# Decoder step with a mixture of experts: the order of a gather and an addition on GpSimd in the periods of the second to fourth expert

## The chip, the cores and the metric

The kernel runs on one core of one Trainium2 chip. The metric is the device time of one execution in microseconds, here the median of several runs of the same kernel. All times come from the profiled execution of the kernel or from those runs. Lines (L749, or line 749) are lines of the kernel file.

## What is computed

The reference is one layer of a hybrid decoder, for a prompt group (512 rows) and a sample group (8 x 4 rows) that share the weights: attention with a window, a short gated convolution and attention over a memory, their normalised concatenation times W_out, and then a mixture of 32 experts of which each row picks four. All of it is float32. What matters here is the last part:

```
h  = x + mix @ w_out
hn = rmsnorm(h)                                  # 544 rows of 1024
gates, experts = softmax(top4(hn @ w_router + b_router))
for each expert e, on the rows that picked it:
    g = hn @ w_gate_up[e] + b_gate_up[e]         # 1024 x 2048, interleaved gate and up
    a = (clip(up, -7, 7) + 1) * gate' * sigmoid(1.702 * gate'),  gate' = min(gate, 7)
    y[row] += gate_of_row * (a @ w_down[e] + b_down[e])
y = rmsnorm(h + y)
```

## The kernel before

The layer up to the router takes the first 250 us or so. Then come 32 experts in order, each with up to 104 rows (a branch with more blocks stands behind a flag and isn't taken here). The rows hn lie in a DRAM table (hn_tbl), and the result is summed up in another (y_tbl), which begins with h.

**A period.** Each expert n has a period, period(n), written out by hand on each engine. Its weights are 12 MB: four chunks of 2 MB for gate and up and two for down, each used as two halves, so 12 halves a period (HALVES). TensorE counts each used half up in `w_used`. Each half is split in two float32r parts, high (ScalarE, high_part, L1133) and low (VectorE, low_part, L1754), and TensorE multiplies three of the four combinations (products, L2435 to L2437). SyncE loads a chunk as soon as TensorE has used up what lay in its buffer. The halves of a period are shifted by two: period n begins with half 2 of expert n and takes in halves 0 and 1 of expert n + 1 as its steps i = 8 and 9. Between the halves TensorE transposes the activations (act_rows, L2430) and, at step 5, the gathered rows of the next expert (x_rows, L2419).

**The rows of an expert.** For the first ten experts the indices of expert n + 2 come from small matrix products (info) at the end of step 9 of period n, and VectorE writes them to idx_i (slot_info, L1721, at step 10). GpSimd then gathers the rows (gather, L749, an indirect DMA of 104 rows of 4 KB). Later experts take the indices from a table. The result of expert n - 1 leaves PSUM on ScalarE at step 0 (y_rows, L1143), and GpSimd adds it to y_tbl by an indirect DMA that adds (scatter, L762). The additions to y_tbl are made one after the other, each behind the landing of the one before, as they may hit the same rows.

**The down offsets.** The offsets b_down are not added expert by expert. For a row tile j of 128 rows (j = 0 to 3; j = 4 has 32) TensorE multiplies the gates of the tile with all experts' down offsets (bias_term, L2482), ScalarE copies the result from PSUM to SBUF (bias_evict, L1270), and GpSimd adds it to y_tbl (add_bias, L814). This happens in the first experts: tiles 0 and 1 before and in period 0, and tile n + 1 in periods n = 1 to 3. Tiles 0, 2, 3 and 4 share one buffer, bias4, so that bias_evict of tile j waits for the addition of the tile before:

```
if j >= 2:
    ac.wait_ge(sem(f"bias_added{0 if j == 2 else j - 1}"), 16)
```

On ScalarE bias_evict(n + 1) stands at step 1 of period n, behind the split of the half of step 4, and ahead of gate_over (L1149) and gate_sigmoid (L1155) of step 2 and of the later splits. On VectorE the product with the sigmoid (swiglu, L1836) waits for gate_sigmoid. TensorE waits for the same bias_evict ahead of step 4 (the term uses a PSUM bank of the transposes). GpSimd's scatter(n) waits for the addition of tile n (n = 1 to 3), and period 4 for that of tile 4.

**GpSimd's own order.** It also spreads the gate and up offsets of the next expert over 128 partitions: bias_rows(n, part), two broadcasts of 512 columns (L682) for each part. They wait for SyncE's load of one row (load_biases, L518), which SyncE issues once ScalarE has written the row before into PSUM (bias_seed, L1171). And in periods 2 to 6 it writes a table of slots with four indirect DMAs a period (table_rows, L733), which the later experts read. slots (L716) copies a column for info.

Of the kernel before, what the change touches and what calls it, by code (L numbers as in the profile page):

```python
# [52 lines left out]
UB = 4  # L53
# [59 lines left out]
def build(nc, x_prompt, x_sample, mem_prompt, cache_win_k, cache_win_v, win_kT, mem_kT, cache_mem_v,  # L113
# [4 lines left out]
    with ctx:  # L118
# [13 lines left out]
        def sem(name):  # L132
            if name not in sems:
                sems[name] = ctx.enter_context(nc.semaphore(name))
            return sems[name]
# [192 lines left out]
        def bias_row(j):  # L328

            return yrow[:, 1, :] if j == 1 else bias4  # L330
# [14 lines left out]
        def row_tile(r):  # L345
            return (memrow[:, r, :], P) if r < 2 else (xrow[0:ROWS[r - 2], r - 2, :], ROWS[r - 2])
# [293 lines left out]
        def _(pool):  # L640
# [6 lines left out]
            for r in range(7):  # L647
                n = row_tile(r)[1]
# [25 lines left out]
            def bias_rows(n, part):  # L674

                pool.wait_ge(sem(("ld_vec_bias0", "ld_mck_bias1")[part]), n * 16 + 32)
                if not isinstance(n, int):
                    seen = cst[0:1, 0:NVC * (3 + part)].rearrange("p (e c) -> p e c", c=3 + part)
                    nc.gpsimd.tensor_copy(arrived[0:1, part:part + 1], seen[:, bass.ds(n, 1), 0])  # L679
                for half in range(2):  # L680
                    cols = slice(part * D + half * 512, part * D + (half + 1) * 512)
                    nc.gpsimd.partition_broadcast(brow[:, cols], brow[0:1, cols], channels=P).then_inc(sem("bias_cast"), 1)  # L682
# [30 lines left out]
            def slots(n, k):  # L713

                wait(pool, "info_pe", counted(n) - 1)
                nc.gpsimd.tensor_copy(rv[:, k % 2], rv_all[:, bass.ds(n, 1)].rearrange("p o j c -> p (o j) c")).then_inc(sem("rv_ready"), 1)  # L716
                pool.wait_ge(sem("rv_ready"), n)
# [8 lines left out]
            def table_rows(first, last):  # L726

                pool.wait_ge(sem("ld_gffn"), 32)
                pool.wait_ge(sem("slot_rows"), 1)
                pool.reg_add(bound, none, CAP * NE - 1)  # L730
                for i in range(first, last):
                    n = ROWS[i // TOPK]
                    nc.gpsimd.indirect_dma_start(  # L733
                        slot_tbl[:, :], bass.IndirectOffsetOnAxis(ap=slot_i[0:n, i:i + 1].bitcast(U32), axis=0),
                        slot_row[0:n, i, :], None, bounds_check=bound, oob_is_err=False).then_inc(sem("table"), 16)

            def table_slots(n, k):

                pool.wait_ge(sem("ld_cst"), 32)
                nc.gpsimd.tensor_copy(idx_i[0:CAP, k % UB:k % UB + 1], slot_sb[0:CAP, bass.ds(n, 1), 0])  # L740
                nc.gpsimd.tensor_copy(gcol[0:CAP, k % UB:k % UB + 1], slot_sb[0:CAP, bass.ds(n, 1), 1]).then_inc(sem("rv_ready"), 1)
                pool.wait_ge(sem("rv_ready"), n)

            def gather(n, k, table=False):

                if not table:
                    pool.wait_ge(sem("idx_ready"), counted(n) + 1)
                pool.reg_add(bound, none, NT - 1)
                nc.gpsimd.indirect_dma_start(  # L749
                    xg[0:CAP, k % 2, :], None, hn_tbl[:, :],  # L750
                    bass.IndirectOffsetOnAxis(ap=idx_i[0:CAP, k % UB:k % UB + 1].bitcast(U32), axis=0),
                    bounds_check=bound, oob_is_err=False).then_inc(sem("gathered"), 16)

            def scatter(n, k):

                pool.wait_ge(sem("yrow_ready"), n * 2)
                if isinstance(n, int) and 0 < n <= 3:
                    for j in ((0, 1) if n == 1 else (n,)):
                        pool.wait_ge(sem(f"bias_added{j}"), 16)
                wait(pool, "scattered", n * 16 - 16)  # L760
                pool.reg_add(bound, none, NT - 1)
                nc.gpsimd.indirect_dma_start(  # L762
                    y_tbl[:, :], bass.IndirectOffsetOnAxis(ap=idx_i[0:CAP, (k - 1) % UB:(k - 1) % UB + 1].bitcast(U32), axis=0),
                    yrow[0:CAP, (k - 1) % 2, :], None,
                    bounds_check=bound, oob_is_err=False, compute_op=ALU.add).then_inc(sem("scattered"), 16)
# [13 lines left out]
            def period(n, k, last=False, table=False, bare=False, overflow=False):  # L779
                old = not (last or table or bare)  # L780
                if old:
                    slots(n + 2, k)
                if not isinstance(n, int) or n > 0:
                    scatter(n, k)
                if not last:
                    if overflow:
                        bias_rows(n + 1, 0)
                    bias_rows(n + 1, 1)
                    pool.wait_ge(sem("w_used"), n * HALVES + 9)
                if isinstance(n, int) and 0 < n < UB:  # L790
                    pool.wait_ge(sem("scattered"), n * 16)
                    add_bias(n + 1)
                if table:
                    table_slots(n + 2, k + 2)
                if old or table:
                    gather(n + 2, k + 2, table)
                if old and not overflow or table:
                    bias_rows(n + 2, 0)
                if old and isinstance(n, int) and 2 <= n < 7:
                    table_rows(4 * (n - 2), 4 * (n - 1))  # L800

# [8 lines left out]
            def add_bias(j):  # L810

                pool.wait_ge(sem("bias_row"), 2 * j + 2)
                pool.reg_add(bound, none, NT - 1)
                nc.gpsimd.indirect_dma_start(  # L814
                    y_tbl[:, :], bass.IndirectOffsetOnAxis(ap=row_i[0:ROWS[j], j:j + 1].bitcast(U32), axis=0),
                    bias_row(j)[0:ROWS[j], :], None,
                    bounds_check=bound, oob_is_err=False, compute_op=ALU.add).then_inc(sem(f"bias_added{j}"), 16)
# [4 lines left out]
            for u in range(2 * UB):  # L822
                if u == UB:
                    pool.wait_ge(sem("bias_added4"), 16)
                period(u, u)
            with pool.Fori(2, NE // UB - 1) as it:
                for u in range(UB):
                    period(it * UB + u, u, table=True)
# [24 lines left out]
            for u in range(UB):  # L853
                period(NE - UB + u, u, u == UB - 1, u < 2, u == 2)
# [1759 lines left out]
```

## Time and profile before

| what | us |
|---|---|
| median of 3 runs (1393.88 to 1400.48) | 1394.35 |
| the profiled execution | 1399.39 |
| its span | 1397.5 |
| TensorE busy in the span | 1359.8 |
| VectorE busy | 1206.0 |
| ScalarE busy | 1070.6 |
| GpSimd busy | 759.1 |

The profile is of one execution. In it period 2 runs from about 331.2 to 366.9 us by TensorE's first and last product, period 4 from 402.6 to 449.1, period 5 to 484.0. In its rows PE is TensorE, PEld its weight loads, DVE VectorE, ACT ScalarE, POOL GpSimd and SP SyncE. A row of a timeline gives the start in us from the span's start, the duration in us, engine, line, operation, output and input tile, the count, and in brackets the idle time before it with what ended that. The landing of a DMA is counted from the start of its issue. Several buffers are parts of one tile named area, so area<-hn_tbl,idx_i is the gather, y_tbl<-area,idx_i the scatter of an expert's result and y_tbl<-area,row_i the addition of a row tile.

### The profile page before, as it was taken

What the parts mean: (1) busy time and instruction counts of PE and PEld (TensorE: products, weight loads), DVE (VectorE), ACT (ScalarE), POOL (GpSimd) and SP (SyncE); (2) the same over time, 40 slices, a digit from 0 to 9 for tenths busy, and PEclk for the clock granted to TensorE, in tenths of its full rate; (3) what the DMA queues carried; (4) which work ended last, traced back from release to release, by engine and by line L of the source; (5) the groups of instructions that cost most, each with busy time, mean ns of one, the idle gap of its engine ahead of it and who ended that gap; (6) DMA issues with size and microseconds to landing.
All of it is one profiled execution on the core that took longest, in us unless ns stands there. A gap on an engine that the chain in (4) does not pass through costs nothing.

```text
span 1397.5 us, 19410 instructions
## 1 busy us (share of the span) xinstructions
PE 1359.8 (97%) x6775; PEld 1000.4 (72%) x6775; DVE 1206.0 (86%) x1098; ACT 1070.6 (77%) x1102; POOL 759.1 (54%) x363
## 2 busy tenths in 40 slices
PE   9999998999997999999999999999999999999995
PEld 6988655667775777777777777777777777777773
DVE  5466555899996999999999999999999999999996
ACT  5354413878885888888888888888888888888884
POOL 2022112386775979656666666566665666665403
PEclk9999999999998999999999999999999999999998
DMA  9522171999997999999999999999999999999984
GB/s 353 196 66 83 75 286 61 367 378 372 388 391 269 363 386 364 366 387 382 381 390 388 369 385 369 382 384 376 383 381 370 383 376 378 391 376 377 383 304 149
DMA packets 52506, 461.48 MB, mean 330 GB/s; under 512 B 11545, under 2 KB 15611, under 8 KB 26825
## 3 DMA queue, kind: packets, MB, share of 16 engines
q1 hardware_dynamic: 40169, 438.59, 80.2%
q0 software_dynamic: 10624, 20.42, 6.5%
q10 hardware_dynamic: 1648, 1.65, 0.4%
q8 instruction: 36, 0.59, 0.2%
q14 instruction: 29, 0.24, 0.0%
HBM read 446.88 MB, written 24.31 MB: 337 GB/s over the span
## 4 chain that ended last, share of the span: by engine, by line
PE 67%; DMA 2%; issue 1%; POOL 1%; DVE 0%; ACT 0%; POOLq 0%; ACTq 0%; DVEq 0%
PE psum L2437 21%; PE psum L2436 21%; PE psum L2435 21%; PE psum L2419 1%; PE psum L2430 1%; DMA area<-hn_tbl,idx_i 1%; POOL small L840 0%; DMA y_tbl<-area,idx_i 0%; POOL brow L682 0%; DVE low L1754 0%; PE psum L2406 0%; DVE ring L1900 0%; POOL out L850 0%; ACT area L1202 0%; ACT ring L1210 0%
## 5 line engine op out<-in xcount | busy, mean ns | idle before, releaser
L1754 DVE TENSOR_TENSOR low<-raw,high 128x2048 fp32r<-128x2048 f32 x384 | 868.2, 2292 | 36.8 <-ACT high L1133 36.7
L1133 ACT CAST high<-raw 128x2048 fp32r<-128x2048 f32 x384 | 727.8, 1912 | 39.0 <-PE psum L2437 35.0
L2435 PE MATMUL psum<-high,area_r 128*104 128x512 f32 x1536 | 610.8, 398 | 3.8 <-DVE area_r L1823 1.5
L2437 PE MATMUL psum<-low,area_r 128*104 128x512 f32 x1536 | 604.7, 394 | 0.0
L2436 PE MATMUL psum<-high,area_r 128*104 128x512 f32 x1536 | 604.3, 393 | 0.0
L2437 PEld LDWEIGHTS psum<-low,area_r 128*104 128x104 f32 x1536 | 258.2, 168 | 96.7
L2435 PEld LDWEIGHTS psum<-high,area_r 128*104 128x104 f32 x1536 | 258.4, 168 | 95.9 <-DVE area_r L1818 2.1
L2436 PEld LDWEIGHTS psum<-high,area_r 128*104 128x104 f32 x1536 | 258.6, 168 | 91.0
L682 POOL PARTITION_BROADCAST brow<-brow x128 | 253.1, 2047 | 27.8 <-issue 15.0
L749 POOL DMA_INDIRECT area<-hn_tbl,idx_i x32 | 173.5, 5423 | 71.7 <-DVE idx_i L1721 42.6
L679 POOL COPY arrived<-cst 1x1 f32 x40 | 84.8, 2121 | 123.0 <-DMA brow<-in_biases 123.0
L762 POOL DMA_INDIRECT y_tbl<-area,idx_i x31 | 110.7, 3571 | 39.1 <-ACT area L1143 27.1
L740 POOL CAST idx_i<-us 104x1 int32 (+1 forms) x22 | 17.8, 807 | 135.9 <-PE psum L2437 135.9
L1159 ACT CAST area_r<-psum 128x416 fp32r<-128x416 f32 x64 | 32.4, 506 | 73.3 <-PE psum L2430 73.3
L659 POOL TENSOR_TENSOR ring<-ring,small 128x512 f32<-128x512 f32 (+2 forms) x18 | 24.2, 1358 | 111.5 <-DVE small L1425 111.5
L1171 ACT COPY psum<-brow 104x512 f32<-104x512 f32 x128 | 75.5, 591 | 0.0
L1149 ACT ACTIVATE area<-psum,cst 104x512 f32<-104x512 f32 x64 | 44.1, 689 | 29.7 <-PE psum L2437 29.7
L733 POOL DMA_INDIRECT slot_tbl<-wr,us x20 | 50.8, 2538 | 5.4 <-issue 5.4
L2196 PE MATMUL psum<-ring,area 128*128 128x512 f32 x112 | 52.4, 601 | 0.0
L1823 DVE TENSOR_TENSOR area_r<-psum,area_r 128x416 fp32r<-128x416 f32 x64 | 37.5, 587 | 15.5 <-ACT area_r L1159 15.4
L1155 ACT ACTIVATE area<-area,cst 104x512 f32<-104x512 f32 x64 | 47.0, 735 | 2.8
L1143 ACT ACTIVATE area<-psum,area 104x512 f32<-104x512 f32 x62 | 39.3, 686 | 12.8 <-PE psum L2437 12.8
(287 smaller groups left out, 1229.5 us busy)
## 6 DMA issues: line engine op xcount, KB each, us to landing
raw<-in_w_gate_up SPq DMA_DIRECT2D x128, 2048.0 KB, 12.2
raw<-in_w_down SPq DMA_DIRECT2D x64, 2048.0 KB, 11.7
ring<-in_w_in SPq DMA_DIRECT2D x7, 1024.0 KB, 16.2
ring<-in_x_prompt SPq DMA_DIRECT2D x8, 512.0 KB, 9.6
ring<-in_w_out SPq DMA_DIRECT2D x7, 512.0 KB, 4.4
ring<-in_w_mem_kv SPq DMA_DIRECT2D x2, 1024.0 KB, 9.4
ring<-in_mem_kT SPq DMA_DIRECT2D x1, 2048.0 KB
ring<-in_cache_mem_v SPq DMA_DIRECT2D x1, 2048.0 KB, 8.4
```

What stands on the lines that cost most here:

```text
L679: nc.gpsimd.tensor_copy(arrived[0:1, part:part + 1], seen[:, bass.ds(n, 1), 0])
L682: nc.gpsimd.partition_broadcast(brow[:, cols], brow[0:1, cols], channels=P).then_inc(sem("bias_cast"), 1)
L733: nc.gpsimd.indirect_dma_start(slot_tbl[:, :], bass.IndirectOffsetOnAxis(ap=slot_i[0:n, i:i + 1].bitcast(U32), axis=0), slot_row[0:n, i, : ...
L749: nc.gpsimd.indirect_dma_start(xg[0:CAP, k % 2, :], None, hn_tbl[:, :], bass.IndirectOffsetOnAxis(ap=idx_i[0:CAP, k % UB:k % UB + 1].bitca ...
L762: nc.gpsimd.indirect_dma_start(y_tbl[:, :], bass.IndirectOffsetOnAxis(ap=idx_i[0:CAP, (k - 1) % UB:(k - 1) % UB + 1].bitcast(U32), axis=0) ...
L1133: nc.scalar.copy(high_w(i), raw_w(t)).then_inc(sem("w_high"), 1)
L1171: nc.scalar.copy(banks[q][0:CAP, :], brow[0:CAP, q * 512:(q + 1) * 512]).then_inc(sem("spare_bias_in"), 1)
L1754: v.tensor_tensor(low_w(t), raw_w(t), high_w(i), ALU.subtract).then_inc(sem("w_low"), 1)
L2196: last = mm(bank[0:n, :], zT[:, t, j * P:j * P + n], wo[t][:, half * 512:(half + 1) * 512], start=(t == tiles[0]), stop=(t == tiles[-1]))
L2435: mm(bank, high, wh, start=start, stop=False, skip_group_check=True)
L2436: mm(bank, low, wh, start=False, stop=False, skip_group_check=True)
L2437: return mm(bank, high, wl, start=False, stop=stop, skip_group_check=True)
```

## The change

In the periods of experts 1, 2 and 3 (0 < n < UB, UB = 4), GpSimd's wait for the landing of scatter(n) and add_bias(n + 1) move from ahead of gather(n + 2) and bias_rows(n + 2, 0) to behind them. They stay ahead of table_rows. The operations, their data and all other engines' programs are the same.

```diff
@@ -787,15 +787,15 @@
                         bias_rows(n + 1, 0)
                     bias_rows(n + 1, 1)
                     pool.wait_ge(sem("w_used"), n * HALVES + 9)
-                if isinstance(n, int) and 0 < n < UB:
-                    pool.wait_ge(sem("scattered"), n * 16)
-                    add_bias(n + 1)
                 if table:
                     table_slots(n + 2, k + 2)
                 if old or table:
                     gather(n + 2, k + 2, table)
                 if old and not overflow or table:
                     bias_rows(n + 2, 0)
+                if isinstance(n, int) and 0 < n < UB:
+                    pool.wait_ge(sem("scattered"), n * 16)
+                    add_bias(n + 1)
                 if old and isinstance(n, int) and 2 <= n < 7:
                     table_rows(4 * (n - 2), 4 * (n - 1))
```

## Rows read from the trace of the kernel before

**Rows 1.** The page, busy us of each engine, share of the span, instructions
```profile
PE 1359.8 (97%) x6775; PEld 1000.4 (72%) x6775; DVE 1206.0 (86%) x1098; ACT 1070.6 (77%) x1102; POOL 759.1 (54%) x363
```
**Rows 2.** Waits of PE, 260 to 560 us: total, times, longest
```profile
PE psum L2419 <- DMA area<-hn_tbl,idx_i: 9.6, 1, 9.6
```
**Rows 3.** Busy us of PE, PEld, DVE, ACT, POOL by stretch; clock, DMA share, GB/s
```profile
331.20:366.90 35.70, 35.70 (x169) 26.22 (x168) 35.63 (x27) 30.82 (x29) 25.41 (x8) 1.00 1.02 373
402.60:449.10 46.50, 36.91 (x165) 27.03 (x164) 34.33 (x26) 29.79 (x27) 24.10 (x13) 0.89 0.85 314
449.10:484.00 34.90, 34.90 (x165) 25.80 (x164) 33.58 (x26) 29.85 (x26) 32.53 (x13) 1.00 0.97 360
```
**Rows 4.** Timeline of PE, 418 to 431 us
```profile
428.77 1.65 PE L2419 MATMUL psum<-cst,area 104*128 104x104 f32 x8 [9.60 <-DMA area<-hn_tbl,idx_i]
```
**Rows 5.** Timeline of POOL, 270 to 470 us
```profile
324.28 1.58 POOL L814 DMA_INDIRECT y_tbl<-area,row_i  x1 [7.26 <-issue]
328.03 2.60 POOL L749 DMA_INDIRECT area<-hn_tbl,idx_i  x1 [2.16 <-DVE idx_i L1721]
332.37 3.73 POOL L682 PARTITION_BROADCAST brow<-brow  x2 [1.74 <-DMA brow<-in_biases]
...
355.06 5.85 POOL L814 DMA_INDIRECT y_tbl<-area,row_i  x1 [4.46 <-PE psum L2437]
363.12 7.38 POOL L749 DMA_INDIRECT area<-hn_tbl,idx_i  x1 [2.20 <-DVE idx_i L1721]
370.54 2.76 POOL L682 PARTITION_BROADCAST brow<-brow  x2
...
386.71 1.78 POOL L716 CAST area_r<-area_r 128x20 fp32r<-128x20 f32 x1
389.35 6.33 POOL L762 DMA_INDIRECT y_tbl<-area,idx_i  x1 [0.86 <-POOL area_r L716]
395.13 5.06 POOL L682 PARTITION_BROADCAST brow<-brow  x2
407.96 3.94 POOL L814 DMA_INDIRECT y_tbl<-area,row_i  x1 [7.76 <-PE psum L2437]
412.20 5.17 POOL L749 DMA_INDIRECT area<-hn_tbl,idx_i  x1 [0.30 <-issue]
```
**Rows 6.** Landings of L814 (x5), L762 (x8), L749 (x8), 265 to 560 us
```profile
DMA to landing us min/median/max: 10.0/13.8/18.3
DMA to landing us min/median/max: 8.7/13.2/17.7
DMA to landing us min/median/max: 13.4/16.0/21.6
```
**Rows 7.** Timeline of DVE, 265 to 460 us
```profile
341.43 0.68 DVE L1836 SCALAR_TENSOR_TENSOR area<-psum,area 104x512 f32<-104x512 f32 x1
...
362.08 0.15 DVE L1721 TENSOR_SCALAR idx_i<-psum 104x1 int32<-104x1 f32 x1
...
375.40 0.68 DVE L1836 SCALAR_TENSOR_TENSOR area<-psum,area 104x512 f32<-104x512 f32 x1
...
396.79 0.15 DVE L1721 TENSOR_SCALAR idx_i<-psum 104x1 int32<-104x1 f32 x1
```
**Rows 8.** Timeline of ACT, 270 to 450 us
```profile
338.07 1.08 ACT L1270 COPY area<-psum 128x512 f32<-128x512 f32 x2 [1.90 <-DMA y_tbl<-area,row_i]
...
339.83 0.73 ACT L1155 ACTIVATE area<-area,cst 104x512 f32<-104x512 f32 x1
...
371.90 1.05 ACT L1270 COPY area<-psum 32x512 f32<-32x512 f32 x2
...
373.63 0.73 ACT L1155 ACTIVATE area<-area,cst 104x512 f32<-104x512 f32 x1
```
**Rows 9.** Timeline of SP, 300 to 380 us
```profile
325.01 0.24 SPq L518 DMA_DIRECT2D brow<-in_biases  x1
...
360.62 0.24 SPq L518 DMA_DIRECT2D brow<-in_biases  x1
```

## The prediction

> **What bounds the kernel now.** I read the shares first. TensorE is busy for 97% of the span [rows 1], so this time is set by TensorE, and only what makes it wait, or what removes a wait, can count. Then I asked for TensorE's waits over the first eight experts: there is one long one, 9.6 us, in which the transposes of gathered rows (line 2419) wait for the gather [rows 2]. Then the table by expert [rows 3]: expert 4 (fifth in order) takes 46.5 us of TensorE's time line, expert 5 takes 34.9. The difference, **11.6 us**, is all that the stretch can give back. It is a little more than the wait, because the granted clock of that stretch is 0.89 of full speed on average: the first transposes after the wait take 1.65 us for eight [rows 4].
>
> Why is this gather late? In period 3 GpSimd reaches the scatter of expert 3 at 389.35, ends the spreading of offsets at 395.13 + 5.06 = 400.19, and then nothing runs until 407.96 [rows 5]. The releaser named there is TensorE, but by the code three waits stand in a row, the last for the scatter's landing: 389.35 + 17.7, the longest landing of line 762 in the experts asked for [rows 6], is 407.05. Only then come the row tile's addition at 407.96 and the gather at 412.20. Its indices had been ready since 396.79 + 0.15 [rows 7]. So 15 us pass between the indices and the gather, and 12.0 of them (400.19 to 412.20) are the wait and the addition that the change moves behind it.
>
> **What the change moves.** No instruction is added or removed. In periods 1, 2 and 3 the wait for the scatter and the addition (its wait, its descriptors, its transfer) go behind the gather and behind two broadcasts, which have waits of their own: the gather waits for the indices that VectorE writes late in the period, the broadcasts for a row of offsets that SyncE loads.
>
> **Period 3, the gain.** GpSimd would be free at 400.2 in the old frame, after the indices. The gather goes out about 11.8 us earlier, lands after the 16.5 us that it took (rows wanted at 428.77 - 9.60 = 419.2; 400.4 + 16.5 = 416.9), 2.3 us ahead of the need [rows 4, 5]. I take the whole 11.6 us as gained; at the longest landing of a gather in the stretch, 21.6 us [rows 6], 2.8 us of wait would stay.
>
> **Periods 1 and 2, the price.** The addition has a customer that the gather doesn't: one buffer (bias4) holds row tile 2, then 3, then 4. ScalarE may write tile 3 (bias_evict, line 1270, at the second step of period 2) only when the addition of tile 2 has landed. This wait shows already, 1.90 us, until 338.07 [rows 8]; the addition went out at 324.28 and took 13.8. In period 3 the same write starts at 371.90 with no idle time shown. Both stand at their edge, so each microsecond by which the addition is later falls on ScalarE nearly whole. Behind the write on ScalarE stand the clip and sigmoid of SwiGLU and all following splits.
>
> *Period 1.* The gather stays where it is, at 328.03, as it was bound by its indices and not by the addition. The broadcasts stay at 332.37, since they wait for the row of offsets (issued by SyncE at 325.01, 7.36 us before [rows 9]), and end at 336.1. The addition goes out at 336.3, 12.0 us later than before. For its landing I take 13.8 us, which is both its own and the median of the five additions [rows 6]: 350.1. The write moves from 338.07 to 350.1. What does that do to the end? VectorE is the one to follow, not TensorE: it is busy 35.63 of 35.70 us in this period [rows 3], so lost time on it isn't made up. Its SwiGLU product starts at 341.43 and needs ScalarE's sigmoid, which ended at 339.83 + 0.73 = 340.56, so 0.87 us is spare [rows 7, 8]. Shift: 350.1 - 338.07 - 0.87 = **11.2 us**. TensorE stops ahead of the fifth of the period's twelve half-chunks (it waits there for the same write, since that shares a PSUM bank), due near 331.2 + 35.7 x 4/12 = 343.1, and again for a split half that ScalarE and VectorE have not made yet.
>
> *Period 2*, all of it 11.2 later. Indices at 362.08 + 11.2 = 373.3, gather at 374.3 (363.12 before), its descriptors 7.38 us, until 381.7; the offsets' row would be there at 360.62 + 11.2 + 7.36 = 379.2, so the gather decides; the broadcasts add 2.76, and the addition goes out at 384.7 [rows 5, 7, 9]. Landing: 13.8 again, 398.5. The write of tile 4 was at 371.90, with 375.40 - 374.36 = 1.04 us spare ahead of VectorE's product [rows 7, 8]. Whole shift by then: 398.5 - 371.90 - 1.04 = **25.6 us**.
>
> *Period 3* pays no third time: no tile comes after 4. Here GpSimd must still be in time: after 384.7 up to 5.9 us of descriptors, the four table scatters (370.54 + 2.76 to 386.71, so 13.4), the slots 1.8, the scatter 6.3 and the broadcasts 5.1, which ends near 418. The indices come at 396.8 + 25.6 = 422.4 [rows 5, 7]: the gather isn't late. Behind it, in period 4, GpSimd first waits for the addition of tile 4; the broadcasts for the next expert then come near to their need, which may cost 0 to 5 us. I take nothing and leave the 5 to the range.
>
> **Sum.** +25.6 - 11.6 = +14.0 us. Against the profiled execution's own time, 1399.39 (span 1397.5 and 1.9 around it), that is 1413.4. The median of the runs is 1394.35, 5.0 less; I carry the difference over: **1408**. The unprofiled runs might hold less of the old wait for the gather than this one does; then the gain is smaller and the result higher.
>
> **The landing of the moved addition is the unknown cost.** With L for it, the two periods give about 2L - 2.0 (13.8 gives 25.6). The nearest rows are 10.0 and 18.3, the shortest and longest addition [rows 6]. At 10.0, with short descriptors of 2.6 us for the gather (that of 328.03) so that the offsets' row decides, the shift is 15.4 and the sum +3.8, 1398. At 18.3 with the same 7.38 it is 34.6 and the sum +23, 1417. I take 13.8, because TensorE's stop does not stop the weights already asked for: in the stop of the old kernel the gather still took 16.5. Break-even is at L = 6.8 us, and no indirect transfer of these experts landed under 8.7.
>
> The Trainium skill has a rule that speaks for a quick landing: "DMA: Bandwidth & Descriptors", section "Anatomy of one DMA — SWDGE (gpsimd) path", fits a GpSimd transfer as 2.0 us plus its bytes over 436 GB/s. For a tile of 128 rows of 4 KB that would be an estimated 3.2 us, and the sum by it -7, or 1387. The trace does not agree: a transfer of this size took 13.8 [rows 6].
>
> **Rivals.**
> - *The addition lands at once, the write is hardly held, and the kernel gets faster.* Place: the wait on line 1270 in periods 2 and 3; price 2L - 2.0; it decides from 6.8 us down. ScalarE reached the write at 338.07 - 1.90 = 336.2 [rows 8], and the addition would have to be down soon after its issue at 336.3; with no hold at all the time is 1394.35 - 11.6 = 1383. Against it: the five additions took 10.0 to 18.3, and the wait is there already. Chance 0.05. The fit of the Trainium skill named above would bring this case about.
> - *The holds come, small.* A TensorE that stops asks for no new weights, so transfers drain and land sooner, as the scatter behind the old stop did in 8.7. 8.7 in both periods: 2 x 8.7 - 2.0 = 15.4, or 12.8 with the quick descriptors, less 11.6, so +1 to +4, and 1397 in the middle. Chance 0.15.
> - *The holds come and the gather stays late*, because the scatter, the table's scatters and the gather share GpSimd's queue. No gain then: +25.6, 1420. For it: gathers up to 21.6 us. Against it: 419.2 - 396.9 = 22 us lie between indices and need. Chance 0.10.
> - My forecast, both holds and the gain: 0.70.
>
> **How the numbers follow.** A difference under 0.5% (7 us) is about what a measurement of this kernel can tell from no change. Faster by more: 0.05. Within: the small holds, most of 0.15, and the lower end of the forecast (L under 11.5): 0.17 together. Slower: 0.78. The range goes from the small holds, 1397, to 1419, nearly the case without a gain and L = 18.3.
>
> **What the profile would show.** Right: ScalarE's line 1270 waits for the DMA of the row addition about 14 us in period 2 (1.9 before) and about 15 in period 3 (0 before), TensorE idle some 8 to 10 us in each, mostly ahead of the fifth half-chunk, and again about 2; VectorE idle 11 to 14 us ahead of line 1836; no wait of line 2419 for the gather; periods 2 and 3 near 47 and 50 us, period 4 near 35; from expert 5 on nothing new. Each step has its row: addition 2 issued near 336, addition 3 near 385, gather 5 within 2 us of its indices. Wrong: additions that land in under 7 us; a line 1270 with no wait; a gather of period 3 that TensorE still waits for.

## The result: slower by 1.4%, and the profile after

| | us |
|---|---|
| kernel before, median of 4 runs (1393.88 to 1400.48) | 1396.37 |
| changed kernel, median of 4 runs (1414.22 to 1416.25) | 1414.88 |
| ratio, 95% interval | 1.0138 (1.0111 to 1.0164) |
| profiled execution after, and its span | 1414.22, 1412.4 |

The forecast was 1408 in a range of 1397 to 1419, slower by 14. The loss is 18.5 us by the medians. The spans of the two profiles differ by 14.9 only, because the profile of before was taken of an execution that was slower than most of that kernel's; the section on the spread comes back to it.

The waits of TensorE in the changed kernel, 260 to 620 us (who waited for whom: total, times, longest), are the first thing to read against [rows 2]:

```profile
PE psum L2435 <- ACT area L1270: 17.8, 2, 9.4
PE psum L2435 <- DVE low L1754: 1.5, 4, 0.7
...
PE psum L2419 <- DMA area<-hn_tbl,idx_i: 0.2, 1, 0.2
```

The wait of 9.6 us for the gather is gone. In its place TensorE waits twice, 17.8 us together, for bias_evict. ScalarE and VectorE in the same stretch of the same kernel:

```profile
ACT area L1270 <- DMA y_tbl<-area,row_i: 28.1, 2, 14.6
...
ACT psum L1171 <- POOL brow L682: 10.3, 2, 6.4
```

```profile
DVE area L1836 <- ACT area L1155: 24.1, 2, 13.4
```

So the chain is the forecast one: the addition of a row tile lands late, ScalarE may not write the next tile into bias4, its sigmoid comes late, and VectorE's product and all splits behind it. The second ScalarE line is new: it twice waits for GpSimd's broadcasts. Now the timeline of GpSimd, 270 to 530 us, with the rows that answer to [rows 5]:

```profile
327.12 2.54 POOL L749 DMA_INDIRECT area<-hn_tbl,idx_i  x1 [11.07 <-DVE idx_i L1721]
330.54 4.57 POOL L682 PARTITION_BROADCAST brow<-brow  x2 [0.88 <-DMA brow<-in_biases]
335.29 1.71 POOL L814 DMA_INDIRECT y_tbl<-area,row_i  x1 [0.17 <-issue]
...
373.50 7.33 POOL L749 DMA_INDIRECT area<-hn_tbl,idx_i  x1 [20.92 <-DVE idx_i L1721]
380.87 2.54 POOL L682 PARTITION_BROADCAST brow<-brow  x2
383.58 3.48 POOL L814 DMA_INDIRECT y_tbl<-area,row_i  x1 [0.17 <-issue]
...
433.64 6.17 POOL L814 DMA_INDIRECT y_tbl<-area,row_i  x1 [0.17 <-issue]
...
446.93 5.42 POOL L733 DMA_INDIRECT slot_tbl<-wr,us  x1 [0.30 <-issue]
452.35 1.91 POOL L716 CAST area_r<-area_r 128x20 fp32r<-128x20 f32 x1
455.13 6.01 POOL L762 DMA_INDIRECT y_tbl<-area,idx_i  x1 [0.87 <-POOL area_r L716]
460.58 1.79 POOL L682 PARTITION_BROADCAST brow<-brow  x2
```

The gather of period 1 did not get earlier: before it started at 328.03 [rows 5], and this execution runs 1 us ahead of the other from period 1 on. Only the addition moved. ScalarE, 325 to 540 us, answers to [rows 8]:

```profile
348.76 1.07 ACT L1270 COPY area<-psum 128x512 f32<-128x512 f32 x2 [13.56 <-DMA y_tbl<-area,row_i]
...
396.48 1.05 ACT L1270 COPY area<-psum 32x512 f32<-32x512 f32 x2 [14.56 <-DMA y_tbl<-area,row_i]
...
461.87 0.59 ACT L1171 COPY psum<-brow 104x512 f32<-104x512 f32 x1 [6.36 <-POOL brow L682]
```

And VectorE, 325 to 420 us, to [rows 7]; the products were at 341.43 and 375.40:

```profile
351.27 0.69 DVE L1836 SCALAR_TENSOR_TENSOR area<-psum,area 104x512 f32<-104x512 f32 x1 [10.74 <-ACT area L1155]
...
398.96 0.69 DVE L1836 SCALAR_TENSOR_TENSOR area<-psum,area 104x512 f32<-104x512 f32 x1 [13.36 <-ACT area L1155]
```

They come 9.8 and 23.6 us later, in an execution that is 1 us ahead. For a balance by period I take the starts of y_rows on ScalarE (L1143) one after the other; where the broadcasts hold ScalarE up, only the sum of two periods means something.

| from one y_rows to the next, us | before | after | difference |
|---|---|---|---|
| period 1 | 37.6 | 37.5 | -0.1 |
| period 2 | 35.6 | 46.7 | +11.1 |
| period 3 | 35.6 | 47.7 | +12.0 |
| periods 4 and 5 | 82.0 | 73.8 | -8.2 |
| periods 6 and 7 | 70.5 | 71.5 | +1.0 |
| sum | | | +15.8 |

With the 1 us by which this execution was ahead at its period 1, that is the 14.9 of the spans. From period 8 on both take 34.6 a period.

### The profile page after: what moved, and what is told of

The parts are those of the page before. It is cut to its first block, busy times and chain, and to the rows that moved or that the text cites. A ratio compares the mean times of both kernels' runs of the same rounds, so it can differ in the third digit from the quotient of the medians.

```text
span 1412.4 us, 19413 instructions
## 1 busy us (share of the span) xinstructions
PE 1366.3 (97%) x6775; PEld 1004.4 (71%) x6775; DVE 1204.7 (85%) x1098; ACT 1069.1 (76%) x1102; POOL 743.5 (53%) x363
## 4 chain that ended last, share of the span: by engine, by line
PE 78%; DVE 9%; issue 4%; POOL 3%; DMA 3%; ACT 2%; SPq 0%; POOLq 0%; ACTq 0%; DVEq 0%
PE psum L2435 20%; PE psum L2437 20%; PE psum L2436 20%; DVE low L1754 5%; PE psum L2196 4%; PE psum L2033 2%; PE psum L2035 2%; PE psum L2034 2%; DMA y_tbl<-area,row_i 2%; PE psum L2430 1%; PE psum L2419 1%; POOL brow L682 1%; POOL slot_tbl L733 1%; DMA ring<-in_x_prompt 1%; ACT high L1133 1%
## 5 line engine op out<-in xcount | busy, mean ns | idle before, releaser
L1754 DVE TENSOR_TENSOR low<-raw,high 128x2048 fp32r<-128x2048 f32 x384 | 865.5, 2285 | 42.5 <-ACT high L1133 42.2
L1133 ACT CAST high<-raw 128x2048 fp32r<-128x2048 f32 x384 | 727.1, 1912 | 34.6 <-PE psum L2437 30.5
L2435 PE MATMUL psum<-high,area_r 128*104 128x512 f32 x1536 | 612.8, 399 | 23.3 <-ACT area L1270 17.8
L682 POOL PARTITION_BROADCAST brow<-brow x128 | 236.0, 1915 | 29.5 <-DMA brow<-in_biases 23.3
L749 POOL DMA_INDIRECT area<-hn_tbl,idx_i x32 | 174.5, 5454 | 112.6 <-DVE idx_i L1721 84.0
L762 POOL DMA_INDIRECT y_tbl<-area,idx_i x31 | 105.0, 3388 | 52.7 <-ACT area L1143 27.1
L740 POOL CAST idx_i<-us 104x1 int32 (+1 forms) x22 | 17.8, 808 | 131.9 <-PE psum L2437 131.9
L1836 DVE SCALAR_TENSOR_TENSOR area<-psum,area 104x512 f32<-104x512 f32 x64 | 43.8, 685 | 24.1 <-ACT area L1155 24.1
L1839 DVE SCALAR_TENSOR_TENSOR area<-area 104x512 f32<-104x512 f32 x64 | 47.3, 740 | 2.2
```

What stands on the lines that cost most here:

```text
L749: nc.gpsimd.indirect_dma_start(xg[0:CAP, k % 2, :], None, hn_tbl[:, :], bass.IndirectOffsetOnAxis(ap=idx_i[0:CAP, k % UB:k % UB + 1].bitca ...
L762: nc.gpsimd.indirect_dma_start(y_tbl[:, :], bass.IndirectOffsetOnAxis(ap=idx_i[0:CAP, (k - 1) % UB:(k - 1) % UB + 1].bitcast(U32), axis=0) ...
L1133: nc.scalar.copy(high_w(i), raw_w(t)).then_inc(sem("w_high"), 1)
L1754: v.tensor_tensor(low_w(t), raw_w(t), high_w(i), ALU.subtract).then_inc(sem("w_low"), 1)
L2435: mm(bank, high, wh, start=start, stop=False, skip_group_check=True)
```

## Experiments

Two theories stood against each other. A is the forecast's: the price is the hold on bias4, twice, and the gain is the gather of period 3. B: moving the addition costs by itself, in GpSimd's queue or by late broadcasts, in each of the three periods alike. Each run has its own runs of the kernel before beside it, with medians of 1393.86, 1393.72 or 1393.43 us; against 1393.86 the whole change costs 21.0 us. All edits are to the lines of the change, against the kernel before, unless said otherwise. In kernels with added lines, bias_evict is L1271, L1273 or L1275 and x_rows L2420 to L2424.

### One period at a time

Period 3 alone:

```diff
-                if isinstance(n, int) and 0 < n < UB:
+                if isinstance(n, int) and 0 < n < 3:
                     pool.wait_ge(sem("scattered"), n * 16)
                     add_bias(n + 1)
...
                     bias_rows(n + 2, 0)
+                if isinstance(n, int) and n == 3:
+                    pool.wait_ge(sem("scattered"), n * 16)
+                    add_bias(n + 1)
```

> Only in period 3 do the wait for the scatter and the addition stand behind the gather and the broadcasts; periods 1 and 2 are as before. Theory A (the price is the hold on bias4 in periods 2 and 3, the gain is the gather of period 3 that is no longer late): no tile comes after 4, so there is no price; line 1270 waits 1.9 us as before, no wait of line 2419 for a gather, and the time is 5 to 11 us below the kernel before (ratio 0.992 to 0.996), less than 11.6 because the broadcasts of period 4 come late behind the addition (the changed kernel shows a wait of 6.4 us on them). Rival B (moving the addition costs by itself, through GpSimd's queue or late broadcasts, in every period alike): a third of the loss stays, ratio 1.00 to 1.005.

Measured: 1388.34 us against 1393.86 for before, ratio **0.9961** (0.9946 to 0.9977). This is faster than both kernels. Its waits of TensorE, 260 to 620 us, hold nothing large:

```profile
PE psum L2438 <- DVE area_r L1821: 0.8, 1, 0.8
PE psum L2438 <- issue: 0.6, 1, 0.6
PE psum L2438 <- DVE area_r L1826: 0.2, 1, 0.2
```

and GpSimd, 320 to 530 us, sends the gather as soon as the broadcasts of 394.57 end, 12.4 us earlier than at 412.20 [rows 5], while the addition waits for the scatter as it did before:

```profile
394.57 5.05 POOL L682 PARTITION_BROADCAST brow<-brow  x2
399.81 2.82 POOL L749 DMA_INDIRECT area<-hn_tbl,idx_i  x1 [0.18 <-issue]
403.26 2.31 POOL L682 PARTITION_BROADCAST brow<-brow  x2 [0.63 <-DMA brow<-in_biases]
407.04 1.81 POOL L817 DMA_INDIRECT y_tbl<-area,row_i  x1 [1.47 <-DMA y_tbl<-area,idx_i]
```

The addition goes out at 407.04, where it had been at 407.96. So in period 3 the move is free: the wait for the scatter's landing, not GpSimd's order, sets the addition. B, which wanted a loss here, is out. Periods 4 and 5 take 70.35 us together and periods 4 to 7 take 140.9, and ScalarE waits for no broadcast there, against the expectation.

Period 1 alone (the conditions are 1 < n < UB ahead and n == 1 behind):

> Only in period 1 is the addition behind the gather and the broadcasts. Theory A: one hold, line 1270 waits about 13.5 us in period 2, TensorE loses 11 us there, the gather of period 3 stays late and its wait of some 10 us stays: ratio 1.006 to 1.010. Rival B: a third of the loss, about +5 us, spread and not ahead of the fifth half-chunk, ratio near 1.004.

Measured: 1400.72 against 1393.86, ratio 1.0049 (1.0032 to 1.0067), which is below the 1.006 to 1.010 that A was given and near the number of B. The place decides: ScalarE's timeline, 330 to 420 us, and the waits of TensorE show one hold where A puts it.

```profile
349.63 1.07 ACT L1273 COPY area<-psum 128x512 f32<-128x512 f32 x2 [12.86 <-DMA y_tbl<-area,row_i]
```

```profile
PE psum L2438 <- ACT area L1273: 7.7, 1, 7.7
...
PE psum L2422 <- DMA area<-hn_tbl,idx_i: 0.7, 1, 0.7
```

Period 2 takes 46.1 us, 10.5 more than in the run with period 3 alone. But the wait for the gather in period 4 is down to 0.7, though that gather was not moved here. GpSimd, 325 to 480 us, shows where it went:

```profile
400.43 6.34 POOL L762 DMA_INDIRECT y_tbl<-area,idx_i  x1 [0.86 <-POOL area_r L716]
...
413.91 2.83 POOL L817 DMA_INDIRECT y_tbl<-area,row_i  x1 [2.63 <-PE psum L2440]
417.04 2.63 POOL L749 DMA_INDIRECT area<-hn_tbl,idx_i  x1 [0.30 <-issue]
```

The scatter of expert 3 is issued 11.1 us later than in [rows 5], like all the rest behind the hold, but it lands after 12.6 us in place of 17.7. So the addition goes out only 6.0 and the gather only 4.8 us later than before, and the gather lands after 13.9 in place of 16.5. Why the scatter landed sooner was not tried. In periods 4 to 7 ScalarE waits twice for broadcasts, 3.8 and 3.9 us, and they take 143.8 us, 2.9 more than with period 3 alone. By the periods this run is 10.5 + 2.9 = 13.3 us behind that one, by the medians 12.4. A had left the wait for the gather standing; that it is nearly gone explains the low ratio.

Period 2 alone (n in (1, 3) ahead, n == 2 behind):

> Only in period 2 is the addition behind the gather and the broadcasts. Theory A: one hold, on the write of tile 4 in period 3. The addition goes out some 17 us later than before (355.1 to about 372), so line 1270 waits 13 to 15 us there, and TensorE loses 11 to 13 us in period 3; from this goes what the wait for the gather of period 4 was worth in the runs (about 4 to 5 us by the run with its own buffer and the old order, and by the run with period 3 alone), as the gather is then no longer in time trouble or is: ratio 1.005 to 1.010. Rival B (a third of the loss for each period): 1.0045. Together with the run of period 1 alone and of period 3 alone the three should add up to the whole change within 5 us, or the periods interact.

Measured: 1405.01 against 1393.72, ratio 1.0084 (1.0055 to 1.0112). The addition went out at 374.77, 19.7 later than in [rows 5], ScalarE's write waited 17.2 us, TensorE 12.1, and no wait for the gather is left. The three ratios add up to +0.49 + 0.84 - 0.39 = 0.94%, 13 us, where the whole change costs 1.38%, 19 us. So the periods interact: the wait for the gather, worth 5.5 us by the run with period 3 alone, can be removed only once, but each of the three runs removes it. Against this, the hold of period 3 is longer when it stands alone: the period takes 50.4 us here and 47.7 in the changed kernel.

### A buffer of its own

```diff
-            return yrow[:, 1, :] if j == 1 else bias4
+            return yrow[:, 1, :] if j == 1 else bias_own if j == 3 else bias4
...
-                if j >= 2:
-                    ac.wait_ge(sem(f"bias_added{0 if j == 2 else j - 1}"), 16)
+                if j in (2, 4):
+                    ac.wait_ge(sem(f"bias_added{j - 2}"), 16)
```

To make room, the two buffers of the slot mask (hot) became one, whose write waits for the product before it, and the tile area grew by 136 columns.

> The changed kernel, with a buffer of its own for row tile 3, so that the write of tile 3 waits for no addition and that of tile 4 for the addition of tile 2 only (one of the two buffers of the slot masks is given up for the room). Theory A: both waits on line 1270 go (0 to 2 us left), periods 2 and 3 return to about 35.7 us, and the gain of period 3 stands alone: ratio to the kernel before 0.991 to 0.997. But GpSimd's scatters 2 and 3 still wait for the additions of tiles 2 and 3, and may hold up broadcasts: up to 5 us of ScalarE waiting for line 682 in place of it. Rival B: the loss stays, ratio 1.010 or more.

Measured on the changed kernel's order: 1388.50 against 1393.86, ratio **0.9963** (0.9944 to 0.9981). The whole loss is gone, with GpSimd's order as in the change. ScalarE, 330 to 380 us, writes both tiles with no idle time ahead:

```profile
336.76 1.07 ACT L1271 COPY area<-psum 128x512 f32<-128x512 f32 x2
...
372.71 1.04 ACT L1271 COPY area<-psum 32x512 f32<-32x512 f32 x2
```

In this run ScalarE waits 4.4 us for broadcasts, 3.9 of them at 403.10, within what was allowed for.

The control, with the order of before:

> Control for the one above: the kernel before with the same separate buffer and the single slot mask. Theory A: the 1.9 us wait on line 1270 goes, which VectorE had covered but for 0 to 1 us, and the late gather stays: ratio 0.998 to 1.002. If it is far from 1, the room that was made costs or gives something by itself, and the run above has to be read against this one.

Measured: 1393.62 against 1393.86, ratio 0.9996 (0.9979 to 1.0014). The buffer by itself gives nothing. So the hold on bias4 is the cause of the loss, shown by taking it away: 1.0138 becomes 0.9963. B is out here too: what late broadcasts cost by themselves is a few us at most.

### What sets the landing of the addition

In all three periods, gather, addition, broadcasts:

```diff
                     gather(n + 2, k + 2, table)
+                if isinstance(n, int) and 0 < n < UB:
+                    pool.wait_ge(sem("scattered"), n * 16)
+                    add_bias(n + 1)
                 if old and not overflow or table:
                     bias_rows(n + 2, 0)
```

> In all three periods the order is gather, wait and addition, broadcasts: the addition is behind the gather but ahead of the broadcasts. Theory A with price 2L - 2.0 less what the addition is earlier: it goes out near 330.8 in place of 335.3 in period 1 (4.5 us earlier) and some 2.7 us earlier in period 2, so the waits on line 1270 shrink by that to about 9 and 8 to 12 us, and the time lies 7 to 10 us below the changed kernel: ratio 1.007 to 1.010. If the gather right ahead of it in the same queue lengthens the landing by the same amount, the ratio stays near 1.013 (rival C: the queue's order sets the landing, not the time of issue).

Measured: 1411.64 against 1393.72, ratio 1.0141 (1.0109 to 1.0173). GpSimd and ScalarE in the period of the first hold:

```profile
328.58 2.53 POOL L749 DMA_INDIRECT area<-hn_tbl,idx_i  x1 [11.06 <-DVE idx_i L1721]
331.42 3.28 POOL L814 DMA_INDIRECT y_tbl<-area,row_i  x1 [0.30 <-issue]
...
349.13 1.07 ACT L1270 COPY area<-psum 128x512 f32<-128x512 f32 x2 [12.49 <-DMA y_tbl<-area,row_i]
```

The addition of tile 2 went out at 331.42, 2.8 us behind its gather, but it landed after 17.7 us, at 349.1. In the changed kernel it went out at 335.29 and took 13.5. With the executions' offset of 1.4 us taken out, 5.3 us of earlier issue brought 1.0 us of earlier landing. My price, 2L - 2.0 with a fixed L, was wrong for this run, and rival C came true. By the medians this order is 3.2 us faster than the changed kernel; A had wanted 7 to 10. The gather ahead landed at 328.58 + 13.2 = 341.8, so 7.3 us lie between the two landings; in the changed kernel 7.8 (gather 341.0). This suggested rule D: about 13 us from the issue, or about 7.5 us behind the transfer ahead in this queue, whichever is later. The test takes the gather from ahead of the addition, but leaves the addition as late:

```diff
+                ahead = isinstance(n, int) and 0 < n < 3
+                if ahead:
+                    bias_rows(n + 2, 0)
+                    pool.wait_ge(sem("scattered"), n * 16)
+                    add_bias(n + 1)
                 if old or table:
                     gather(n + 2, k + 2, table)
```

(period 3 as in the change)

> Periods 1 and 2: broadcasts, wait and addition, then the gather; period 3 as in the changed kernel. So the addition is as late as in the changed kernel but has no gather ahead of it in GpSimd's queue. Theory D (a transfer of this queue lands about 13 us after its issue, or about 7.5 us after the one ahead of it, whichever is later; it fits the landings of the changed kernel and of the run with the addition right behind the gather): addition 2 goes out near 335.5 and lands near 348.5, the wait on line 1270 stays at 12 to 14 us in period 2, and about 11 to 13 in period 3, where the gather no longer stands between; ratio 1.010 to 1.014. Rival C (the gather ahead in the queue makes the landing late): addition 2 lands 5 to 7 us sooner, near 342, the waits shrink to 6 to 8 us, ratio 1.002 to 1.006.

Measured: 1405.29 against 1393.43, ratio 1.0091 (1.0060 to 1.0121), between the two. GpSimd, 320 to 450 us, and ScalarE, 330 to 420 us, tell them apart:

```profile
335.30 1.70 POOL L819 DMA_INDIRECT y_tbl<-area,row_i  x1 [0.17 <-issue]
337.30 1.43 POOL L749 DMA_INDIRECT area<-hn_tbl,idx_i  x1 [0.30 <-issue]
...
376.58 3.29 POOL L819 DMA_INDIRECT y_tbl<-area,row_i  x1 [0.18 <-issue]
```

```profile
349.35 1.07 ACT L1275 COPY area<-psum 128x512 f32<-128x512 f32 x2 [14.17 <-DMA y_tbl<-area,row_i]
...
389.61 1.05 ACT L1275 COPY area<-psum 32x512 f32<-32x512 f32 x2 [7.10 <-DMA y_tbl<-area,row_i]
```

In period 1 no other transfer of the queue is under way when the addition goes out, and it still took 14.0 us from 335.30; the hold stays at 14.2. C fails there, and the landing is the one of D. In period 2 the addition went out 7.0 us sooner than in the changed kernel, because it need not wait for the gather's indices and its 7.33 us of descriptors; it took 13.0, and the hold shrank from 14.6 to 7.1. The ratio lies under what was expected of D, since I had overlooked that period 2 gets its addition out earlier; 7 us off the changed kernel's 1.0138 is 1.0088, and 1.0091 was measured.

D is fitted to these rows and is no law of the queue. In the kernel before, the addition of 355.06 took 16.8 us (to 371.88) and the scatter of 389.35 took 17.7, though the landing ahead of theirs in this queue lay over 15 us back; both kept GpSimd busy for about 6 us, which the landing includes, as it is counted from the start of the issue.

### Period 3 alone, with the addition ahead of the broadcasts

> Period 3 alone, with the order gather, addition, broadcasts. Theory A: like the run with period 3 alone and the addition behind the broadcasts, since the scatter's landing near 407 sets the addition in both: ratio 0.995 to 0.998. The broadcasts of period 3 then wait for 407 and end near 414; their customer, the seed of the next expert, comes at about 414 too, so up to 2 us may be lost.

Measured: 1389.99 against 1393.72, ratio 0.9974 (0.9956 to 0.9992): the order within period 3 makes no difference that these intervals can tell. Its profile has a small one: ScalarE waits twice, 3.9 us each, for broadcasts, and periods 4 to 7 take 142.9 us in place of 140.9; the medians differ by 1.7.

### The spread of the kernel before

> The kernel before once more, for a second profile. The runs of before so far spread over 1388 to 1401. Theory: the spread is the length of the wait for the gather in period 4, 9.6 us in the first profile (1399.4) and 3.6 in that of the own buffer with the old order (its span 1393.3). A profile with a time near 1394 should show 3 to 5 us, one near 1399 8 to 10. Rival: the spread is elsewhere (clock, the layer's first part), and the wait is 9 to 10 us whatever the time.

Measured: 1394.36 against 1393.72, ratio 1.0002 (0.9982 to 1.0022). The profiled execution took 1395.40, and TensorE's wait for the gather, 260 to 620 us, is not 9.6 but:

```profile
PE psum L2419 <- DMA area<-hn_tbl,idx_i: 3.8, 1, 3.8
```

Its GpSimd rows, 320 to 450 us, show what differs: the addition and the gather take 1.40 and 2.48 us on GpSimd in place of 3.94 and 5.17 [rows 5], and the gather landed after 13.8 us in place of 16.5.

```profile
408.01 1.40 POOL L814 DMA_INDIRECT y_tbl<-area,row_i  x1 [7.26 <-issue]
409.71 2.48 POOL L749 DMA_INDIRECT area<-hn_tbl,idx_i  x1 [0.30 <-issue]
```

The row with 7.26 us idle is the same wait for the scatter that the first profile put down to TensorE. Three profiles of the old order, with waits of 9.6, 3.8 and 3.6 us, go with 1399.39, 1395.40 and 1395.14. No execution of this kernel near 1388, the lower end of the spread, was profiled.

Why GpSimd takes twice the time for the same issue in some executions was not tried. But the traces show what goes with it: how much of VectorE's split of the weights (low_part, L1754) falls into the issue. Here are the second of four table scatters and VectorE beside it in the kernel before, and then the first of the four in the changed kernel, where VectorE was idle from 385.6 to 399.0:

```profile
376.71 5.36 POOL L733 DMA_INDIRECT slot_tbl<-wr,us  x1 [0.30 <-issue]
376.73 4.49 DVE L1754 TENSOR_TENSOR low<-raw,high 128x2048 fp32r<-128x2048 f32 x2
...
387.37 1.02 POOL L733 DMA_INDIRECT slot_tbl<-wr,us  x1 [0.30 <-issue]
```

All four of the changed kernel took 0.97 to 1.02 us, and the gather of 462.56, again with VectorE idle, 1.12. In the first profile the addition of 407.96 started 0.4 us ahead of a split, at 408.37, and took 3.94; in the second it started 0.9 us ahead of it (408.01 and 408.92) and took 1.40. That the split holds GpSimd up is argued from this, not tried.

## Why the prediction was right, and where its numbers were off

The mechanism was the forecast one: two holds on bias4 as the price, the late gather of period 3 as the gain. That the sum came out near is partly luck: the holds were put too high by 2.5 us, which made up for a part of the gain put too high by 6.1 and of the late broadcasts, 4.4, put at nothing, and in the first comparison the kernel before happened to stand 2.5 us above its later median.

- **The gain of period 3**, put at 11.6 us with its wait of 9.6: right in kind (the wait is 0.2 us after, and none is left in the run with period 3 alone), too large as a term. By the runs it is 1393.86 - 1388.34 = 5.5 us. The step that failed is "all that the stretch can give back", read from one execution that was slower than most. The text had said that other runs might hold less of this wait and the result be higher. They did, and it was: of the terms that were off this is the largest. The loss exceeds the forecast's 14.0 by 4.5 us in the first comparison, and the measured time exceeds its 1408 by 6.9.
- **Period 1 and the first hold**: addition out at 336.3 (335.3 measured, in an execution 1 us ahead), landing after 13.8 (13.5), shift 11.2 (11.1 by the period). Following VectorE and not TensorE gave the right number: TensorE idles 8.4 us, the period loses 11.1.
- **Period 2 and the second hold**: gather 374.3 (373.50), addition 384.7 (383.58), landing 13.8 (12.9). The further shift was put at 14.4 and is 12.0. Of the 2.4 us between, 0.9 are the landing; at VectorE's product the whole shift is 24.5 (375.40 to 398.96, and the 1 us ahead), and by the end of the period it is 23.1, so 1.4 us were made up behind it, which the sum had ruled out.
- **Both holds** 25.6, measured 23.1. The landing was the right unknown, and 13.8 a good value; but as a constant it was wrong. It would have mispriced an addition close behind the gather by some 4 us, as the run with that order showed.
- **Late broadcasts**, given 0 to 5 us and put at nothing: ScalarE waits 6.4 and 3.9 us for them, and against the run with period 3 alone periods 4 and 5 cost 73.8 - 70.35 = 3.4 and periods 6 and 7 cost 1.0. The chain is in GpSimd's rows above: addition at 433.64, table scatters until 452.35, scatter at 455.13, broadcasts at 460.58, ScalarE at 461.87. This is a term of 4.4 us that belonged in the sum; the forecast's "period 4 near 35" and "from expert 5 on nothing new" failed by it (40.3 us in period 4, 37.9 in period 6). It doesn't need the two holds: the run with period 2 alone shows 2.0 us of it, and so does the one of period 3 alone with the addition ahead of the broadcasts, which has no hold at all.
- **Together** with the typical gain: 23.1 + 4.4 - 5.5 = 22.0. By the runs it is 21.0 against the 1393.86 that the kernel before took in the median of the larger set of runs in the first experiments, from which the 5.5 comes. In the first comparison the kernel before stood at 1396.37; from there the gain would be 1396.37 - 1388.34 = 8.0 and the sum 19.5, and 18.5 was measured. The balance closes within 1 us either way; the periods' numbers are those of single executions.
- **The rivals.** A landing too quick to hold anything, which the fit of the Trainium skill ("DMA: Bandwidth & Descriptors", section "Anatomy of one DMA — SWDGE (gpsimd) path") would bring about: no. The two moved additions of 128 rows in the changed kernel took 13.5 and 12.9 us, four times its estimated 3.2. Small holds: no, the stop of TensorE did not make them land sooner. In both stops, 342 to 349 and 390 to 397 us, the DMA engines were still fully busy (the last three columns are granted clock, DMA share and GB/s):

```profile
342.00:349.00 7.00, 0.00 (x0) 0.00 (x0) 0.00 (x0) 0.24 (x1) 0.00 (x0) 0.67 1.02 365
349.00:355.00 6.00, 5.11 (x14) 3.59 (x15) 3.59 (x3) 5.91 (x7) 2.87 (x3) 0.54 0.81 286
390.00:397.00 7.00, 0.00 (x0) 0.00 (x0) 0.00 (x0) 0.52 (x2) 2.16 (x3) 0.65 1.02 351
```

  The quicker landing that this rival counted on did come, but only behind the stops: the scatters of 349.71 and 397.45 landed after 7.6 and 6.3 us. The late gather: no, TensorE waited 0.2 us for it.

## What to carry to other kernels

Ahead of moving a transfer back in a queue, list who waits for its landing, buffers that are used again above all, and look whether such a wait shows already: one of 1.9 us says that there is no slack left but what the engines behind it have (0.87 us here). The same edit can be free in one period and dear in the next (here -5.5 us in period 3, about +7 and +11 us in periods 1 and 2, each run alone), so apply it where its customer is absent, or give the customer a buffer: both versions beat both kernels, at 0.996 of the time before. And a stall that ends with the landing of a transfer can differ from execution to execution (9.6, 3.8 and 3.6 us here), so the gain of removing it should be read from more than one profile.

## What the runs showed that I had not expected

- The moved additions of 128 rows, beside a full load of weights, landed 12.7 to 14.2 us after their issue, or 7 to 8 us behind a transfer close ahead where that was later: 341.8 and 349.1, and with period 2 alone 383.0 and 390.3 (15.5 us). Issues of 6 us on GpSimd took 16.8 and 17.7. A transfer beside a thinner load was quicker: the gather issued at 462.56 in the changed kernel took 5.4 us, in a stretch in which the engines moved 156 GB/s:

```profile
462.00:468.00 6.00, 5.29 (x24) 3.62 (x23) 3.56 (x3) 6.00 (x7) 5.61 (x5) 1.00 0.66 156
```

- After the stop TensorE's granted clock is 0.54 of full speed in the mean over 349 to 355 us (row among the rivals), so mostly its lower level of 1.2 GHz, and the first products take 0.75 and 0.63 us in place of 0.39. Ahead of it TensorE had been idle for 8.4 us:

```profile
349.89 0.75 PE L2435 MATMUL psum<-high,area_r 128*104 128x512 f32 x1 [8.42 <-ACT area L1270]
```

  It cost next to nothing, as VectorE and ScalarE were behind anyway: the shift of VectorE, 341.43 to 351.27 and the 1 us ahead, 10.8, is that of the period within 0.3.
- A hold in an early period removed most of a wait two periods on (0.7 us in place of 3.8), as the scatter that the late gather stood behind landed 4.6 us sooner than in the second profile of before (12.6 and 17.2). Runs that each undo one part therefore don't add up to the whole.
